# ScalarE takes over all copies of turned prompt probabilities from VectorE, and TensorE turns the first head's groups on that head's exponential

## The reference, cut to what matters

```
s = q k^T / 8 - slope * distance      # masked to the union of three dilated windows
p = exp(s - max(s)); den = sum(p)
o = (p v) / den
```

## Time and profile before

| what | value |
|---|---|
| median of 3 runs | 2818.22 us (2817.1 to 2826.28) |
| the profiled execution | 2819.52 us, its span 2817.5 us |
| granted TensorE clock over the span | 0.981 |
| busy: PE, DVE, ACT, POOL | 2689.4, 1803.5, 895.4, 106.0 us |
| the attention stage | about 1494 to 1962 us of the span |

### The profile page before, as it was taken

The page is one execution under the profiler, slowest core; times in us unless marked ns, Lnnn a source line. Parts: engine busy times, 40 slices in busy tenths (PEclk is TensorE's granted clock), DMA queues, the critical chain, the costliest instruction groups (busy, mean ns, idle before and its releaser), DMA issues.

```text
span 2817.5 us, 55417 instructions
## 1 busy us (share of the span) xinstructions
PE 2689.4 (95%) x23897; PEld 2574.9 (91%) x23897; DVE 1803.5 (64%) x2910; ACT 895.4 (32%) x1598; POOL 106.0 (4%) x233
## 2 busy tenths in 40 slices
PE   7999999999999999999998887778999999999998
PEld 7999999999999999999996665556999999999998
DVE  5755537777676677755525666666368777767666
ACT  5544524222222222432223333335233222222222
POOL 1010000000000000000021111100000000000000
PEclk9999999999999999999998899999999999999999
DMA  5120220111111111223278888884101111111112
GB/s 198 45 69 18 95 75 16 46 46 46 46 46 46 60 46 46 109 92 94 89 215 242 211 203 224 219 228 147 60 31 32 60 46 46 46 46 46 46 60 79
DMA packets 160385, 254.59 MB, mean 90 GB/s; under 512 B 10897, under 2 KB 132965, under 8 KB 159632
## 3 DMA queue, kind: packets, MB, share of 16 engines
q1 hardware_dynamic: 146624, 189.04, 23.3%
q0 software_dynamic: 12208, 57.48, 6.4%
q10 hardware_dynamic: 1312, 4.52, 0.5%
HBM read 222.98 MB, written 28.02 MB: 89 GB/s over the span
## 4 chain that ended last, share of the span: by engine, by line
PE 85%; DVE 9%; ACT 2%; issue 2%; DMA 1%; SPq 0%; ACTq 0%; POOL 0%; DVEq 0%
PE psum L1575 30%; PE psum L1630 17%; PE psum L484 14%; PE psum L225 11%; PE psum L1550 3%; PE psum L2529 3%; DVE smp_kt L2662 2%; DVE att_scores L2739 2%; PE psum L2496 2%; PE psum L2481 2%; PE psum L2447 1%; DVE att_pt L2684 1%; PE psum L2556 1%; DMA x_natural<-in_x_prompt 1%; PE psum L593 1%
## 5 line engine op out<-in xcount | busy, mean ns | idle before, releaser
L1811 DVE TENSOR_TENSOR x_res<-x_res,psum 128x544 f32<-128x544 f32 x352 | 250.5, 719 | 154.8 <-PE psum L1630 154.8
L484 PE MATMUL psum<-w_hi,h_hi 128*128 128x256 f32 (+1 forms) x1152 | 326.7, 284 | 1.0 <-ACT qkv_tok L2075 1.0
L484 PE MATMUL psum<-w_hi,h_lo 128*128 128x256 f32 (+1 forms) x1152 | 323.6, 281 | 0.0
L484 PE MATMUL psum<-w_lo,h_hi 128*128 128x256 f32 (+1 forms) x1152 | 322.9, 280 | 0.0
L1630 PE MATMUL psum<-ffn_hi,ffn_unit_hi 128*128 128x272 f32 x1408 | 292.6, 289 | 1.8 <-DVE x_res L1811 1.6
L1630 PE MATMUL psum<-ffn_lo,ffn_unit_hi 128*128 128x272 f32 x1408 | 291.5, 288 | 0.0
L1630 PE MATMUL psum<-ffn_hi,ffn_unit_lo 128*128 128x272 f32 x1408 | 290.7, 288 | 0.0
L1575 PE MATMUL psum<-h_hi,ffn_unit_lo 128*128 128x272 f32 x1280 | 265.2, 288 | 0.0
L1575 PE MATMUL psum<-h_lo,ffn_unit_hi 128*128 128x272 f32 x1280 | 264.8, 288 | 0.0
L1575 PE MATMUL psum<-h_hi,ffn_unit_hi 128*128 128x272 f32 x1280 | 264.5, 288 | 0.0
L1630 PEld LDWEIGHTS psum<-ffn_hi,ffn_unit_hi 128*128 128x128 f32 x1408 | 220.7, 188 | 3.2 <-DVE x_res L1811 3.2
(11 more groups left out here) (387 smaller groups left out, 5212.3 us busy)
## 6 DMA issues: line engine op xcount, KB each, us to landing
cache_tile<-in_cache_k SPq DMA_DIRECT2D x320, 128.0 KB, 8.6
cache_tile<-in_cache_v SPq DMA_DIRECT2D x64, 512.0 KB, 12.7
w_raw<-in_w_ffn_gate SPq DMA_DIRECT2D x22, 1024.0 KB, 5.1
w_raw<-in_w_ffn_up SPq DMA_DIRECT2D x22, 1024.0 KB, 5.1
w_raw<-in_w_ffn_down SPq DMA_DIRECT2D x22, 1024.0 KB, 4.9
w_raw<-in_w_in_att SPq DMA_DIRECT2D x12, 1024.0 KB, 7.1
w_raw<-in_w_in_rec SPq DMA_DIRECT2D x10, 1024.0 KB, 5.0
park_x<-x_res POOLq DMA_DIRECT2D x2, 4368.0 KB, 13.3
```

The costliest lines, as they stand in the source:

```text
L484: mm = pe.matmul(PS[0:n, bank, 0:BW], st[:, k, w:w + n], mv[slot][:, k * BW:(k + 1) * BW], start=(k == 0 and x == 0) if used is None else ...
L1811: dve.tensor_tensor(x, x, pset(dset(g, i)), ALU.add).then_inc(s_res, 1)
```

## The change

ScalarE takes every unit "p"; VectorE's branch for them goes. The units "p" of TensorE wait for one exponential of the block where all four tiles of the group belong to the first head, and for both otherwise. The order of the lists is not edited, but as ScalarE has more units, other ones fall into `mine[0:2]` and `mine[2:4]`: in the slots with n % 8 = 7 and 0 (four groups) two copies stand before the first exponential and two between the exponentials, where before both of ScalarE's stood ahead of the first.

```diff
     def by_act(unit):
 
-        return unit[0] not in ("p", "s") or unit[0] == "s" and unit[2] == 1 or unit[0] == "p" and unit[2] % 8 == 4
+        return unit[0] not in ("p", "s") or unit[0] == "s" and unit[2] == 1 or unit[0] == "p"
 
...
             elif what == "p":
-                pe.wait_ge(a_p, 2 * x + 2)
                 blocks = x % QT + 1
+                pe.wait_ge(a_p, 2 * x + 1 if c + 4 <= blocks else 2 * x + 2)
...
                 dve.wait_ge(t_in[TB_[g]], TC_[g])
-                if what == "p":
-                    k = min(4, 2 * (x % QT + 1) - c)
-                    op = dve.tensor_copy(PT[:, x % 2, c:c + k, :].rearrange("p a w -> p (a w)"), bank[:, 0:k * P])
-                elif c < 2:
+                if c < 2:
```

## The result

The changed kernel took 2787.62 us (median of 4 runs, 2785.02 to 2788.28), the kernel before 2818.54 in the same comparison (4 runs, 2817.1 to 2826.28): a ratio of 0.9883, interval 0.987 to 0.9897. So 31 us are gained, where 65 were forecast. The direction was right and the size was not. 2787.6 lies at the slow end of the range (2728 to 2788), and only because the range had been stretched over the middle of rival B; the forecast's own range, 2741 to 2768, was missed by 20 us.

What follows compares the result with a forecast made beforehand. No engine is full; hand-overs bound the attention stage, chiefly TensorE waiting for VectorE's copies. With loads limiting next, 56 in the pairs plus 9 behind gives 65 us gained, 2753 us; own range 2741 to 2768, 8 in 10: 2728 to 2788.

Steps and rivals of the forecast that it cites:

- rival B: ScalarE's in-order list delays copies, so TensorE's waits only halve and clock stays partly low: 2786 us; chance 0.25.
- The waits for the copies: Attention stage: TensorE's 22 waits for VectorE's copies, 58.2 us in all, would end, worth 7.9 us a pair.
- The clock: Three slow stretches behind TensorE's waits would run at full clock, returning 5.9 us a pair of heads.
- The loads: Six steady pairs: DMA engines are late next, at 258 GB/s 51.2 us a pair, so 56 us gained.
- ScalarE's order: ScalarE's new copies, as an order in its list, would cost 1.5 us a pair, bounds 0 and 3.0.
- (a): TensorE still waits 0.2 to 0.3 us for the first copy before its third group in three slots: 0.8 a pair.
- (b): Slots n % 8 = 7 and 0: third and fourth copies stand behind the first exponential, priced at 0.2 us a pair.
- (c): Slots 1 and 2 of eight: a copy ahead of the second exponential delays the denominators' copy, showing as about 0.5 us.
- The ends: Behind the six steady pairs, the seventh pair's slot 7 and the last pair gain 9 us; ahead, nothing.
- rival D: ScalarE becomes last link of each slot, moved copies costing 0.6 us each: 24 us lost, 2842 us; chance 0.06.
- A: Loads keep up at 275 GB/s or more, so a pair costs 48.1 us: 2731 us; chance 0.17.
- C: Waits on VectorE become equally long waits on ScalarE or on late tiles; nothing moves, 2818 us; chance 0.04.

Runs made afterwards that it cites:

- before_half: The kernel before, with every cache tile but the first in each buffer loading only half its columns: 2813.91 us.
- pv64: The changed kernel with the product of probabilities and values in 64-wide instead of 32-wide pieces: 2763.10 us.
- after_half: The changed kernel, with every cache tile but the first in each buffer loading only half its columns: 2735.92 us.
- dve12_half: The changed kernel on halved cache loads, with VectorE keeping the copies of the slots with one and two blocks: 2731.90 us.
- wait_only: The kernel before with only the weaker wait on exponentials, VectorE's old copies kept: 2821.22 us.
- before_pv64: The kernel before with the product of probabilities and values in 64-wide instead of 32-wide pieces: 2820.81 us.

## Why the prediction was half right

| us | tiles in full | tiles halved |
|---|---|---|
| before | 2818.5 | 2813.9 |
| changed | 2787.6 | 2735.9 |
| changed, 64-wide products | 2763.1 | 2732.5 |

**The waits for the copies**: right. 7.9 a pair were forecast, 7.5 went (48.9 -> 4.0 in six), 8.0 on halved tiles. The remainder of 0.2 to 0.3 per slot is 0.25. As said, they name ScalarE and are under 15 us. Slots 5 and 7 of the eight came out as short as in the kernel on halved loads (6.33 and 7.05) wherever no hole fell into them.

**The clock**: wrong, and this is the larger part of the miss. 5.9 a pair were to come back. In the changed kernel none did (busy 284.35 -> 284.78, clock 0.90 -> 0.90, where 0.95 or more was to be seen). On halved loads 3.6 a pair came back (262.63), or 4.2 against before_half (287.75), in pv64 2.7. The step that failed is the silent assumption that no other idle stretch would put the clock down again. In the changed kernel it fell behind issue waits (0.51 behind the one of 3.58) and in slot 3 of all six pairs. The size was too high as well: 5.9 was read from one pair, and six times 5.9 is 35 us, while a clock of 0.90 over 362.5 us leaves 36 to be won at most, from every idle stretch there is. The prediction's sentence that the rows disagree with the Trainium skill's loop goes too far: its matrix instructions follow without a pause, and here TensorE waited 2.0 to 3.4 us for the copy. "The low clock stays although the waits are gone" was named as a way to be wrong, and it is the one that came.

**The loads**: the bound was there, but it was not what was late next. The step "the DMA engines are late next" counted only cache tiles as what suffers from full engines. The kernel before had 11.6 us of issue waits of TensorE in its six pairs, in the view of waits that was read, and the sum left them where they were, with no reason given. With the other waits gone they doubled to 22.9, the longest 3.6 us, and held the pairs at 55.7 us before tiles could hold them at 51.8. With the holes taken away (pv64), the forecast of this step is met: 51.8 for 51.2, a share of 1.03 for 1.0, waits at L2556 and L2662 of 20.5 us in six pairs, 3.4 a pair, for "a few us a pair". Part of this match is luck: the rate was 247 GB/s and not 258, and this window moves 76.68 MB and not 79.30. With the bytes taken away instead, a pair is 48.4 for 48.1. That match is in part luck too: 3.6 instead of 5.9 by the clock, and 1.4 of issue waits gone that the forecast hadn't counted (11.6 -> 3.5 in six).

**ScalarE's order**: a little too cheap. (a) holds, 0.25 in three slots. (b) can't be read by itself. (c) was 0.5 a pair, which is what slots 1 and 2 show together, 0.34 (in after_half) and 0.16, though slot 2 was to carry it. Slot 3 wasn't priced and took up to 0.9, by the clock. In the whole kernel it is 4.0 us from after_half to dve12_half, within their spread. The row that the earlier trace rows answer to, `att_out` in slot 2 of the changed kernel:

```profile
1736.06 0.29 DVE L2768 TENSOR_TENSOR att_out<-psum,att_rden_rows 128x128 f32<-128x128 f32 x1 [1.04 <-ACT att_rden_rows L2642]
```

It now waits 1.04 us where it waited for nothing, but 0.16 of this is lost time.

**Engine loads**: VectorE's busy time fell by 54.9 (1803.5 -> 1748.6; forecast 61.3), ScalarE's rose by 41.3 (895.4 -> 936.7; forecast 53.9). ScalarE's copies now run in twos: 128 and 32 of them, where 595 and 376 ns each would give 88.2 us, show 83.7 as busy. So part of the difference is overlap that the sum of durations counted twice.

**The ends**: 9 behind the pairs were forecast, 4.5 came. There ScalarE is the last link, in a small way what rival D described: VectorE's waits between 1877.4 and 1940 are

```profile
DVE att_out L2768 <- ACT att_rden_rows L2642: 25.7, 10, 5.4
```

and slot 2 of the last pair takes 4.77 us where it took 3.55, slot 7 8.06 for 7.11. With the copies of dve12_half slot 2 is back at 3.56; slot 7 stays at 8.06. Ahead of the pairs nothing was to change, and 1.4 were lost; the last slot ahead of them took 12.1 us before and 16.4 after, but also 16.0 in wait_only and 15.5 in before_pv64, which have the old copies, so no cause is shown.

The sum again, forecast against profile: pairs 56 against 28, end 9 against 4.5, start 0 against -1.4.

**The rivals.** A (loads keep up) is out: the pairs ran at 234 GB/s and a share of 0.94, and in pv64, where nothing else held them, at 247 and 1.03. B's time, 2786, is the measured one, but its mechanism isn't: it asked for over 25 us of waits on ScalarE's copies, and there are 4.4 in the stage. A time that fits is no proof of a mechanism. C is out: 44.9 us of waits for copies went, and 4.0 came back under ScalarE's name. D is out as a whole. Waits of `att_out` on L2642 rose from 15.5 to 82.4 us, in the six pairs from 7.8 to 56.7 (the longest, 9.1 us, covers the hole of 3.58). But 42.3 of them stay in the pairs of after_half, which are short: they come of the new order, and nearly all is idle time of VectorE that costs nothing.

**The best version that ran** is pv64, 2763.1 us: 57.7 under its own kernel without the change and 24.5 under the changed one, with tiles as its bound.

What stays open: when a packet of instructions is asked for, and so how long it waits for its turn, and why a wait of about two microseconds is followed by the low clock in one pair and not in the next.

## What to carry to other kernels

When an edit removes waits from a stage with full DMA engines, look at the "issue" waits of the engine that it speeds up before you sum: the profile names no cause for them, they lie partly hidden behind the waits that you remove, and they can grow. Lay the packets of the instruction queue beside them: if each ends right behind a landing, the engine waits for its own list. Price the clock's return only if every idle stretch of that size goes. And where a stage has many small matrix instructions, fewer and wider ones may cost the same array time and still win, once nothing else hides how they arrive.

## What had not been expected of the hardware

- TensorE stood still for up to 3.6 us, also inside an accumulation, with the DMA engines at 1.03: issue waits of 22.9 us in six pairs; 3.5 with the tiles halved and 0.8 with 64-wide products. All 79 in 13 traces stand at the border between two packets of 256 instructions and end 1.18 to 1.71 us behind a landing.
- 64-wide products cost what twice as many 32-wide ones cost: 56 of the 32-wide take 1.74 us, 28 of the 64-wide 1.75, both at the full clock.
- The kernel before pays 6.4 us for half of its tile bytes, the changed one 51.7, 64-wide 30.6: how dear a transfer is depends on what else is waiting.
- The low clock followed a wait of 1.95 us (0.56) and did not follow one of 2.41 (1.00).
